# Two blocks of a transformer on one core: activation halves side by side in the first feed-forward matrix

## The reference, cut to what matters

```
def swiglu(x, w_in, w_out):
    a, b = jnp.split(x @ w_in, 2, axis=-1)      # w_in: 1024 x 5632, w_out: 2816 x 1024
    return (jax.nn.silu(a) * b) @ w_out

for l in range(DEPTH):                          # DEPTH = 2, in both block types
    x = x + 0.5 * swiglu(rmsnorm(x, ffn1_norm[l]), w_ffn1_in[l], w_ffn1_out[l])
    ...                                         # three attention or recurrence branches
    x = x + 0.5 * swiglu(rmsnorm(x, ffn2_norm[l]), w_ffn2_in[l], w_ffn2_out[l])
```

## Time and profile before

| | |
|---|---|
| median of three runs | 3194.67 us |
| profiled execution, its own time | 3195.8 us |
| its span | 3194.0 us |
| TensorE matmuls busy | 2976.2 us, 93% |
| VectorE busy | 1690.8 us, 53% |
| ScalarE busy | 1364.8 us, 43% |
| matmuls of the first matrices, L838 | 3 x 2816 |
| matmuls of the second matrices, L858 | 3 x 1408 |
| mean granted TensorE clock | 0.958 |

### The profile page before, as it was taken

How to read it: one execution, slowest core, us unless ns; L and a number is a source line. 1 busy time by engine, 2 the same in 40 slices (tenths; PEclk the granted TensorE clock), 3 DMA queues, 4 the chain that set the end, 5 groups by cost and what they waited for, 6 DMA issues and landing times.

```text
span 3194.0 us, 49255 instructions
## 1 busy us (share of the span) xinstructions
PE 2976.2 (93%) x21202; PEld 2781.6 (87%) x21202; DVE 1690.8 (53%) x2846; ACT 1364.8 (43%) x1928; POOL 6.5 (0%) x10
## 2 busy tenths in 40 slices
PE   5998989999999889999999998999999989899997
PEld 5998778899998878899899986789989989677997
DVE  6656532466665843266665334446666533444665
ACT  4435442244444534244443344534444333553443
POOL 0000000000000000000000000000000000000000
PEclk9999989999999899999999898999999988899998
DMA  6543354555555243455456642255555465225553
GB/s 198 181 156 116 106 145 132 172 185 185 185 163 163 69 132 106 144 186 180 150 185 181 188 130 67 80 158 185 174 167 184 143 182 131 82 68 157 172 182 99
DMA packets 493384, 476.49 MB, mean 149 GB/s; under 512 B 63312, under 2 KB 476528, under 8 KB 493040
## 3 DMA queue, kind: packets, MB, share of 16 engines
q1 hardware_dynamic: 489744, 462.85, 47.0%
q0 software_dynamic: 3424, 10.49, 1.2%
HBM read 467.01 MB, written 6.29 MB: 148 GB/s over the span
## 4 chain that ended last, share of the span: by engine, by line
PE 85%; DVE 8%; ACT 4%; DMA 2%; issue 1%; SPq 0%; DVEq 0%; ACTq 0%
PE ps L767 34%; PE ps L838 32%; PE ps L858 16%; DVE WL L1523 2%; PE ps L939 2%; PE ps L915 1%; DMA RAW<-in_w_in 1%; PE ps L798 1%; ACT WH L1219 1%; DMA RAW<-in_ffn_wi 1%; DVE U L1505 1%; DVE U L1506 1%; DMA RAW<-in_w_ffn_in 1%; ACT REGION L1288 0%; DVE UL L1540 0%
## 5 line engine op out<-in xcount | busy, mean ns | idle before, releaser
L1523 DVE TENSOR_TENSOR WL<-RAW,WH 128x2048 fp32r<-128x2048 f32 (+1 forms) x342 | 761.5, 2234 | 504.1 <-ACT WH L1219 502.2
L1219 ACT ACTIVATE WH<-RAW 128x2048 fp32r<-128x2048 f32 (+1 forms) x342 | 633.3, 1859 | 268.4 <-DMA RAW<-in_ffn_wo 112.6
L838 PE MATMUL ps<-UH,WH 128*128 128x256 f32 x2816 | 406.9, 286 | 44.8 <-ACT WH L1219 24.3
L767 PE MATMUL ps<-REGION,RAW 128*128 128x256 f32 (+3 forms) x1904 | 395.4, 369 | 30.1 <-DVE REGION L2016 13.1
L767 PEld LDWEIGHTS ps<-REGION,RAW 128*128 128x128 f32 (+2 forms) x1904 | 338.5, 190 | 85.4 <-issue 14.8
L838 PEld LDWEIGHTS ps<-UH,WH 128*128 128x128 f32 x2816 | 367.9, 193 | 51.0 <-issue 29.2
L838 PE MATMUL ps<-UH,WL 128*128 128x256 f32 x2816 | 397.5, 284 | 9.3 <-DVE WL L1523 9.3
L858 PE MATMUL ps<-HH,WH 128*128 128x256 f32 x1408 | 395.8, 281 | 2.4 <-DVE WL L1523 2.4
L838 PE MATMUL ps<-UL,WH 128*128 128x256 f32 x2816 | 396.9, 284 | 0.0
L858 PE MATMUL ps<-HH,WL 128*128 128x256 f32 x1408 | 395.4, 281 | 0.0
L858 PE MATMUL ps<-HL,WH 128*128 128x256 f32 x1408 | 395.1, 281 | 0.0
(11 more groups left out here) (212 smaller groups left out, 3045.8 us busy)
## 6 DMA issues: line engine op xcount, KB each, us to landing
RAW<-in_w_ffn_in SPq DMA_DIRECT2D x88, 1024.0 KB, 5.1
RAW<-in_ffn_wi SPq DMA_DIRECT2D x88, 1024.0 KB, 5.1
RAW<-in_w_in SPq DMA_DIRECT2D x86, 1024.0 KB, 5.4
RAW<-in_w_ffn_out SPq DMA_DIRECT2D x32, 1024.0 KB, 5.2
RAW<-in_ffn_wo SPq DMA_DIRECT2D x32, 1024.0 KB, 5.2
RAW<-in_w_out SPq DMA_DIRECT2D x16, 1024.0 KB, 5.2
RAW<-in_w_ffn_out SPq DMA_DIRECT2D x16, 768.0 KB, 4.4
RAW<-in_ffn_wo SPq DMA_DIRECT2D x16, 768.0 KB, 4.5
```

The source lines that it names most:

```text
L767: last = nc.tensor.matmul(o, a, b, start=i == 0, stop=i == len(terms) - 1)
L838: last = nc.tensor.matmul(bank(n, 0, T), a[:, k, side * P:(side + 1) * P], b[:, k, :], start=i == 0 and k == 0, stop=i == 2 and k == DK - 1)
L1219: nc.scalar.activation(part_high(s), raw[pl.place[s]][:, 0:pl.words[s]], ACT.Copy).then_inc(weights_high, 1)
L1523: v_.tensor_tensor(part_low(s), raw[pl.place[s]][:, 0:pl.words[s]], part_high(s).bitcast(FP), ALU.subtract)\
```

## The change

UH and UL become the two halves of one tile, UHL, so that for each of the 8 feature tiles the 256 columns of the high part and the 256 of the low part are adjacent. From the second slab of each first matrix on, TensorE runs one matmul of WH against both (512 columns, the whole bank) and one of WL against UH (256 columns, the bank's first half). The first slab stays as it was. The bank then holds two sums: columns 0 to 255, and columns 256 to 511 (WH x UL). ScalarE copies the second half into TMP's free columns 256 to 511 (`tails`), and VectorE adds it to the first half out of PSUM, then multiplies by RSTD in a second instruction.

```diff
-        UH, UL = sb("UH", [P, DK, T], FR), sb("UL", [P, DK, T], FR)
+        UHL = sb("UHL", [P, DK, 2, T], FR)
+        UH, UL = UHL[:, :, 0, :], UHL[:, :, 1, :]
...
+        tail_out = sem("tail_out")
...
                         opening = j == side == 0
+                        if j > 0:
+                            for k in range(DK):
+                                cols = slice(side * P, (side + 1) * P)
+                                both = (wh[:, k, cols], UHL[:, k, :, :], bank(n, 0, 2 * T))
+                                tail = (wl[:, k, cols], UH[:, k, :], bank(n, 0, T))
+                                for a, b, o in (both, tail) if k < DK - 1 else (tail, both):
+                                    last = nc.tensor.matmul(o, a, b, start=k == 0 and a is both[0], stop=k == DK - 1 and a is both[0])
+                            last.then_inc(product_done, 1)
+                            continue
...
+                def tails(n):
+
+                    for side in range(2):
+                        wait_product(act, n + side)
+                        nc.scalar.activation(TMP[:, side, T:2 * T], bank(n + side, T, 2 * T), ACT.Copy).then_inc(tail_out, 1)
+
                 feed.to(s0 + 1)
                 for j in range(FK // 2):
                     n = p0 + 4 * j + (j > 0)
                     feed.to(s0 + 2 * j + 2)
                     if j == 0:
                         norm_x(first[name + ".norm"])
+                    else:
+                        for side in range(2):
+                            wait_evicted(act, n - 2 + side)
+                        tails(n)
                     for side in range(2):
                         wait_evicted(act, n + side)
                         nc.scalar.activation(SILU[:, side, :], SILU[:, side, :], ACT.Silu).then_inc(gate_done, 1)
                     feed.to(s0 + 2 * j + 3)
+                    tails(p0 + 4 * j + 3)
                     hidden_parts(j)
...
-                def scaled(dst, n):
-
+                def scaled(dst, n, tail=None):
+
+                    if tail is not None:
+                        dve.wait_ge(tail_out, tally.add("tail_out") + 1)
+                        link(v_.tensor_tensor(dst, bank(n, 0, T), tail, ALU.add))
+                        v_.tensor_tensor(dst, dst, RSTD[:], ALU.mult).then_inc(evicted[n % BANKS], 1)
+                        return
                     wait_product(dve, n)
...
                     for side in range(2):
-                        scaled(SILU[:, side, :], n + side)
+                        scaled(SILU[:, side, :], n + side, TMP[:, side, T:2 * T] if j > 0 else None)
                     if j > 0:
                         hidden_parts(j - 1)
                     n = p0 + 4 * j + 3
-                    scaled(TMP[:, 0, 0:T], n)
+                    scaled(TMP[:, 0, 0:T], n, TMP[:, 0, T:2 * T])
                     feed.to(s0 + 2 * j + 3)
-                    scaled(TMP[:, 1, 0:T], n + 1)
+                    scaled(TMP[:, 1, 0:T], n + 1, TMP[:, 1, T:2 * T])
```

## The result

| | before | after |
|---|---|---|
| median of four runs | 3195.16 us | 3328.36 us (3326.8 to 3330.06) |
| ratio | | 1.0418, interval 1.0405 to 1.043 |
| span of the profiled execution | 3194.0 us | 3325.0 us |
| TensorE matmuls busy | 2976.2 us, 93% | 2999.4 us, 90% |
| VectorE, ScalarE busy | 1690.8, 1364.8 us | 1827.7, 1461.5 us |

What follows compares the result with a forecast made beforehand. PE looked like the bound, but a DVE-ACT ring of 10.83 us a pair lay just under its 11.4; 2.45 more makes 13.28, delaying each block 16.7 us, eight 134: 3330 us, range 3290 to 3380.

Steps and rivals of the forecast that it cites:

- The ring before: DVE and ACT handing work to each other, 10.83 us per pair of slabs against PE's 11.4; margin 0.6 us.
- The terms 0.91, 1.08 and 0.46: Additions per pair, in us: SILU evictions 0.91, TMP side 0 1.08, TMP side 1 0.46; sum 2.45, giving 13.28.
- the second term: TMP side 0: odd slab's WL waits for ACT's tail copy and the two-step eviction, 1.08 us more per pair.
- PE's saving is worth nothing: First matrix, slabs 1 to 21: PE's shorter 10.72 us a pair becomes 2.6 us of PE idle time.
- The sum for a block, 140.0: First SILU eviction to second matrix's second weight part takes 140.0 us after the change; delay 16.7 us a block.
- The 123.3 before: First SILU eviction to second matrix's second weight part, in the kernel before the change: 123.3 us.
- the stage: Stretch from a block's first SILU eviction to PE's start on the second matrix's second part, forecast 140.0 us after the change.
- 134: Forecast delay in us over all eight feed-forward blocks, from 16.7 us each.
- 0.216 for the wide matmul: PE's spacing in us of 512-column fp32r matmuls, taken from plain fp32 records; upper bound 0.238.
- rival 1: PE stays the bound and the change pays: 59 us less, 3137 us; chance 0.05.
- The semaphore between two VectorE operations: On DVE, dependent 256-column operations start 0.46 us apart against 0.33 without a semaphore; the Trainium skill says no extra cost.
- rival 3: PE's clock falls in the new stalls: 27 us more, 3357 us, or 3400 if it falls repeatedly; chance 0.12.

Runs made afterwards that it cites:

- the two-step run: Kernel before, each eviction in two dependent VectorE instructions (slab 0's gate stays single), no tails, narrow matmuls: 3236.03 us, ratio 1.0136.
- a tail in front of one single-step eviction: Changed kernel with all tail copies and their waits kept, but each eviction one multiply, the addition left out: 3180.33 us, ratio 0.9957.
- the second term traded for what replaces it: Two runs on the changed kernel: WL moved ahead of the first TMP eviction, 3298.70 us; odd slab's tail copies moved ahead of WH, 3289.24 us.
- the runs with PE as the bound: Changed kernel without tails and second VectorE step, 3179.23 us; without that step only, 3180.33; with ScalarE's order rewritten, 3177.83.
- a third less for TensorE: Changed kernel with the product WL x UH left out of slabs 1 to 21: 3334.90 us, ratio 1.0444.
- the run with wide matmuls alone: Changed kernel without tail copies, each eviction one multiply, WH x UL left out of the result: 3179.23 us, ratio 0.9951.
- The remedy: Changed kernel with ScalarE's order rewritten so WH runs a slab ahead, sums complete: 3177.83 us, ratio 0.995.

## Why the prediction was right, step by step

- *The ring before, 10.83 us, margin 0.6.* Right, and shown by the two-step run: 1.39 us more per pair in a kernel with a margin of 0.6 cost 41 us.
- *The terms 0.91, 1.08 and 0.46.* Right: 13.28 worked out, 13.28 measured. The runs take them apart (in brackets what was expected): the first and third together give 12.22 (12.20); a tail in front of one single-step eviction, which is the second term in part, 11.43 (11.46); the second term traded for what replaces it 13.01 (13.0) and 12.76 (12.74).
- *PE's saving is worth nothing.* Right, and more than was said: a third of its matmuls away is worth nothing either.
- *The sum for a block, 140.0.* Right: 140.04 to 140.06 in all eight. The 123.3 before was a little high, 123.1 on average, so a block is delayed by 17.0 us and not 16.7, eight by 135.8. The spans of the two profiled executions differ by 131.0, since the stretches outside the stage were 4.8 us shorter in all, which nothing in the prediction says. That 134 met the 133 of the medians to 1 us is therefore partly luck; the mechanism and its size in the stage are not.
- *0.216 for the wide matmul.* Wrong: 0.235, close to the upper bound of 0.238. PE's idle time is not 2.6 us a pair but 13.28 - 11.3 = 2.0: 0.4 us before the even slab and 1.6 before the odd one, where the prediction had 0.7 and 1.9. The price of rival 1, 59 us, was too high for the same reason: the runs with PE as the bound lie 14 to 17 us under before, 10.6 of them in the stage. The time of the changed kernel didn't depend on it, since the ring covered it.
- *The semaphore between two VectorE operations.* The addition and the multiply that depends on it start 0.45 to 0.46 us apart in the changed kernel, a multiply and the next instruction that waits for nothing 0.34. The Trainium skill, VectorE: DVE Perf Modes, section The DRAIN you can't avoid, says that the semaphore between two such operations costs nothing extra; by an estimate from it the ring would be 12.9. The 13.28 measured decides against it here.
- *The clock.* The granted clock was 1.00 through stalls of 1.3 us, as forecast, and 0.87 with stalls up to 3.3 us in the run with a third less for TensorE. There the eight stages took no longer for it, but PE had a third less to do, so what a fall would cost with all of the matmuls (27 us and more by rival 3) wasn't measured.

## What to carry to other kernels

Two helper engines that hand work to each other in fixed order form a ring; add it up from start to start, through one period, and compare it with the bound engine's period before adding a step, however idle both helpers look. What counts is the place in the order. The 336 copies alone lengthen the ring by 0.60 us a pair to 11.43, level with TensorE's 11.3 to 11.4: they cost nothing. The second VectorE step alone lengthens it by 1.39 and costs 41 us. Together they lengthen it by 2.45, not 1.99, since the late tail brings the first TMP eviction, now two steps long, into the ring as well: 133 us. The remedy was not less work but moving the producer of the weights ahead of the two waits.

## What was not expected of the hardware

At full clock an fp32r matmul is spaced 0.118 us for 256 columns and 0.235 for 512 in the changed kernel, 0.46 ns a column for both, and 0.231 for 512 on average in the run with wide matmuls alone (a third less for TensorE). At the half clock, in stretches of that run, fp32r is spaced 0.213 for 256 and 0.427 for 512 columns, 0.83 ns a column, which is one column per cycle of 1.2 GHz. One column per cycle of 2.4 GHz would be 0.107 and 0.213, so at full clock fp32r takes 8 to 11% more than that. Plain fp32 records of 256 columns take 0.427 at the half clock, the same as 512 columns of fp32r, but 0.216 at full clock, where they are only 1% over. So the excess of fp32r shows only at 2.4 GHz and goes with the columns, not with the number of instructions, which is why joining two matmuls into one saves next to nothing. What holds it is open. VectorE and ScalarE don't seem to: the wide matmul's mean spacing in the changed kernel is 234 to 235 ns whether VectorE, ScalarE or both work beside it. Stretches without DMA were not looked at apart.
